# Moving four activation tensors in SBUF: split activations placed right behind the weight rings

## The reference, cut to what matters

```python
for i in range(DEPTH):
    g = norm_g[i]
    x = x + 0.5 * rmsnorm(swiglu(rmsnorm(x, g[0]), ffn1_wg[i], ffn1_wu[i], ffn1_wd[i]), g[1])
    xn = rmsnorm(x, g[2])
    ...                                   # y = the layer's mixer of xn
    x = x + rmsnorm(y, g[3])
    x = x + 0.5 * rmsnorm(swiglu(rmsnorm(x, g[4]), ffn2_wg[i], ffn2_wu[i], ffn2_wd[i]), g[5])

def swiglu(x, wg, wu, wd):                # D_MODEL 1024, D_FF 2816
    return (jax.nn.silu(x @ wg) * (x @ wu)) @ wd
```

## Time and profile before

| | |
|---|---|
| time, median of 3 runs | 2140.94 us (2139.95 to 2141.46) |
| span of the profiled execution | 2140.2 us |
| granted TensorE clock, mean over the span | 0.997 |
| TensorE matmuls, busy | 2108.0 us (98%), 14636 instructions |
| VectorE, busy | 1185.7 us (55%) |
| ScalarE, busy | 965.4 us (45%) |
| DMA, mean over the span | 180 GB/s |

### The profile page before, as it was taken

How to read it: one execution, slowest core, us unless ns; L and a number is a source line. 1 busy time by engine, 2 the same in 40 slices (tenths; PEclk the granted TensorE clock), 3 DMA queues, 4 the chain that set the end, 5 groups by cost and what they waited for, 6 DMA issues and landing times.

```text
span 2140.2 us, 35887 instructions
## 1 busy us (share of the span) xinstructions
PE 2108.0 (98%) x14636; PEld 1931.7 (90%) x14636; DVE 1185.7 (55%) x1346; ACT 965.4 (45%) x1177; POOL 52.5 (2%) x100
## 2 busy tenths in 40 slices
PE   8999999999998999999999999999999999999998
PEld 6998989988998998997999899898999899898997
DVE  5555765456456554555645654555645654576543
ACT  5444544344435544454444543554444543544442
POOL 0000000000000000000000000000000000000000
PEclk9999999999999999999999999999999999999999
DMA  8554655546554342342644545453644555455551
GB/s 317 185 191 167 221 185 203 206 160 216 194 185 172 124 153 100 119 158 94 232 186 179 206 187 203 153 193 134 231 185 178 205 188 203 154 212 187 205 187 60
DMA packets 55981, 386.27 MB, mean 180 GB/s; under 512 B 6592, under 2 KB 7104, under 8 KB 10816
## 3 DMA queue, kind: packets, MB, share of 16 engines
q1 hardware_dynamic: 52416, 372.53, 47.2%
q10 hardware_dynamic: 3456, 12.13, 1.6%
HBM read 383.58 MB, written 1.05 MB: 180 GB/s over the span
## 4 chain that ended last, share of the span: by engine, by line
PE 98%; ACT 1%; DVE 0%; issue 0%; DMA 0%; POOL 0%; POOLq 0%; ACTq 0%; DVEq 0%
PE ps L407 29%; PE ps L409 29%; PE ps L408 29%; PE ps L420 2%; PE ps L423 2%; PE ps L426 2%; PE ps L687 1%; PE ps L712 1%; PE ps L700 1%; PE ps L442 1%; PE ps L689 0%; PE ps L674 0%; PE ps L714 0%; ACT xT_high L905 0%; PE ps L497 0%
## 5 line engine op out<-in xcount | busy, mean ns | idle before, releaser
L1219 DVE TENSOR_TENSOR w_low<-raw,w_high 128x2048 fp32r<-128x2048 f32 x352 | 804.2, 2289 | 321.3 <-ACT w_high L881 321.1
L407 PE MATMUL ps<-xT_high,w_high 128*128 128x256 f32 x2656 | 736.0, 277 | 0.0
L409 PE MATMUL ps<-xT_high,w_low 128*128 128x256 f32 x2656 | 734.9, 277 | 0.0
L408 PE MATMUL ps<-xT_low,w_high 128*128 128x256 f32 x2656 | 734.5, 277 | 0.0
L881 ACT ACTIVATE w_high<-raw 128x2048 fp32r<-128x2048 f32 x352 | 670.7, 1911 | 37.7 <-DMA raw<-stream 21.1
L408 PEld LDWEIGHTS ps<-xT_low,w_high 128*128 128x128 f32 x2656 | 499.4, 188 | 2.7
L407 PEld LDWEIGHTS ps<-xT_high,w_high 128*128 128x128 f32 x2656 | 499.0, 188 | 3.1
L409 PEld LDWEIGHTS ps<-xT_high,w_low 128*128 128x128 f32 x2656 | 498.6, 188 | 0.0
L916 ACT ACTIVATE region<-ps 128x256 f32<-128x256 f32 x176 | 67.6, 384 | 668.6 <-PE ps L409 651.3
L407 PE MATMUL ps<-w_high,oT_hi 128*128 128x512 f32 x832 | 330.4, 397 | 0.0
L409 PE MATMUL ps<-w_high,oT_lo 128*128 128x512 f32 x832 | 329.6, 396 | 0.0
(11 more groups left out here) (147 smaller groups left out, 1258.3 us busy)
## 6 DMA issues: line engine op xcount, KB each, us to landing
raw<-stream SPq DMA_DIRECT2D x352, 1024.0 KB, 4.8
gain<-gains ACTq DMA_DIRECT2D x23, 512.0 KB, 4.7
x<-x_in SPq DMA_DIRECT2D x2, 512.0 KB, 6.0
out<-x SPq DMA_DIRECT2D x2, 512.0 KB, 2.6
gain<-gains SPq DMA_DIRECT2D x1, 512.0 KB, 5.3
att_mask<-att_mask_in SPq DMA_DIRECT2D x1, 384.0 KB, 5.1
rope<-rope_in SPq DMA_DIRECT2D x1, 128.0 KB, 4.5
ml_mask<-ml_mask_in SPq DMA_DIRECT2D x1, 128.0 KB, 4.9
```

What stands on the lines that cost most here:

```text
L407: nc.tensor.matmul(acc, lh, rh, start=start, stop=False)
L408: nc.tensor.matmul(acc, lh, rl, start=False, stop=False)
L409: return nc.tensor.matmul(acc, ll, rh, start=False, stop=stop)
L1219: nc.vector.tensor_tensor(w_low[:, p % RING, :], raw[:, p % RAW, :], w_high[:, p % RING, :], ALU.subtract).then_inc(piece_split, 1)
```

## The change

The four `sb` calls of the split activations are moved up, right behind the two rings. Nothing else is touched: every instruction, wait and loop stays as it is, and only addresses differ.

```diff
         w_high = sb("w_high", [P, RING, PIECE], F32R)
         w_low = sb("w_low", [P, RING, PIECE], F32R)
 
+        xT_high = sb("xT_high", [P, KD, SEQ], F32R)
+        xT_low = sb("xT_low", [P, KD, SEQ], F32R)
+        oT_hi = sb("oT_hi", [P, KD, SEQ], F32R)
+        oT_lo = sb("oT_lo", [P, KD, SEQ], F32R)
         x = sb("x", [P, TILES, D])
...
         minus_half = sb("minus_half", [P, 1])
-        xT_high = sb("xT_high", [P, KD, SEQ], F32R)
-        xT_low = sb("xT_low", [P, KD, SEQ], F32R)
         ident = sb("ident", [P, P])
...
         gate_bias = sb("gate_bias", [P, 2 * NH])
-
-        oT_hi = sb("oT_hi", [P, KD, SEQ], F32R)
-        oT_lo = sb("oT_lo", [P, KD, SEQ], F32R)
```

## The result

| | before | after |
|---|---|---|
| time, median of 4 runs | 2140.44 us (2139.72 to 2141.46) | 2178.68 us (2177.45 to 2179.35) |
| ratio after / before, 95% interval | | 1.0175 (1.0162 to 1.0188) |
| span of the profiled execution | 2140.2 us | 2176.6 us |
| granted TensorE clock, mean | 0.997 | 0.997 |

The changed kernel is 1.75% slower. I had forecast 2127 us and a range up to 2172; the time lies above both.

What follows compares the result with a forecast made beforehand. TensorE's matmuls, busy 2108.0 of 2140.2 us, were taken to bound the kernel as a sum of pitches. Down kind -13.5 us, all else 0, gave 2126.7 for the profiled execution, stated as 2127; range 2106 to 2172.

Steps and rivals of the forecast that it cites:

- Block kind: 7968 matmuls streaming 256 columns of `xT` over stationary weights: stays at 113.3 ns, 0 us.
- all turn slow: Upper bound for the 7968 block matmuls: each 4.5 ns slower, 35.9 us more.
- The four steps of 120 ns: Block kind's first four steps after a down product, 0.48 us before settling; cited for rival C.
- down kind: 2496 matmuls, 512 weight columns streaming, `oT` stationary: 234.2 to 228.8 ns, 13.5 us less; lower bound 226.6 ns.
- token kind: 2256 matmuls, 256 weight columns streaming, `xT` stationary: stays slow, 0 us; bounds 10.2 us less to 0.
- early kind: 768 matmuls, 512 weight columns streaming, `xT` stationary: stays at 228.8 ns, 0 us; bounds 1.7 less to 4.1 more.
- VectorE, ScalarE, clock: Engines writing `xT` and `oT` at new places: 0 cost, over 40% of span free; clock was full in every slice.
- Rival C: Load and stream meet at a common start, holding the block kind slow: 2175 us, or 2162 with down gain; chance 0.30.
- Rival A: Common starts settle everything: down and early kinds at 226.6 ns, token kind fast; 30.9 us less, 2110 us; chance 0.16.
- Rival B: Nothing changes; the down kind's 5.4 ns belong to something other than the offset: 2140.9 us; chance 0.20.
- the skill's rule: TensorE never waits on another SBUF user and weight loads take no read bandwidth, so no address can matter.

Runs made afterwards that it cites:

- e1: Kernel before with only `oT` moved behind the rings (`xT` offset 192, `oT` 0): 2149.36 us, ratio 1.0043 to before.
- e3: Changed kernel with pads ahead of `xT` and `oT`, putting `xT` at offset 192 and `oT` at 0: 2150.46 us, ratio 1.0043 to before.
- e2: Kernel before with only `xT` moved behind the rings (`xT` offset 0, `oT` 352): 2195.53 us, ratio 1.0251 to before.
- t_e1: e1 plus one float32 transpose between a down product and the following block at 64 places: 2130.81 us, ratio 0.9952 to before.
- best_both192: Changed kernel with one 192-byte pad ahead of `xT`, so `xT` and `oT` both sit at offset 192: 2132.10 us, ratio 0.9964 to before.
- t_after: Changed kernel plus one float32 transpose between a down product and the following block at 64 places: 2187.52 us.

## Why the prediction was wrong

**The step that failed** is "Block kind, 7968 matmuls, nearly all at 113.3 ns: left at that, 0, since the two paces come with one address and the address alone does not pick." It measured +47.9 us. The observation in it is right, both paces do come with one address, and e1 shows that the stream ahead picks between them; the conclusion is not. The offset decides which paces there are to pick from: 113.3 and 117.8 ns at 192, but 120.0 ns only at 0, in 332 of 332 halves. My bound above fell with it: "all turn slow", 35.9 us, took the slowest pace seen for the slowest there is, though I had written three paragraphs earlier that no pair in the trace starts in common. The four steps of 120 ns on coming from `down` were no warning of it: over all 64 such places the first four average 118.0, and they do settle. No row of the trace before gave the price of 6.7 ns.

**The down kind** went as forecast, and further: -13.5 us forecast, -16.1 measured (-17.7 in e1), a steady 226.7 ns in place of 228.8. That is the lower bound I gave, 226.6, and 19 us less would go with it; the changed kernel gets 16.1, in good part because the first five steps behind a block take 27 ns more than the steady pace there, and nothing more in e1. The direction, the 391 ns and the reason (offset of the stationary tensor) held; e1 and e3 show it.

**The token kind** was given 0 and bounds from -10.2 to 0. It took +5.4, since 117.8 became 120.0, outside the bounds for the same reason. Some 0.4 of this is on 144 matmuls of `arriving` with 256 columns, which my sum had left out.

**The early kind**: 0 forecast, -0.8 measured, inside its bounds; its steady pitch fell from 228.9 to 226.7 like the down kind's. **VectorE, ScalarE, clock**: no change, as said; the four terms make the whole span.

**Rival C** (2162 or 2175, chance 0.30) had the place and the sign. Its price was too small: 4.5 ns where 6.7 were paid. Its reason, that a load and a stream meet because they start in common, is not borne out: offsets 96 and 128 cost the block kind as much. **Rival A** (everything settles) had the 512-column kinds right and the 256-column kinds with the wrong sign. **Rival B**, and with it my reading of the skill's rule as one by which no address can matter, is out: only addresses differ, and the ratio is 1.0175 (1.0162 to 1.0188).

**A coupling that no case of mine had** shows in e1: the gain of the down kind costs the block kind its fast pace. Even with `xT` left alone my number would have been wrong: 2149, not 2127. The forecast comes nearest to the layout 192 and 192 (2132.10; -11.8 us on the down kind), which takes the down kind only to 228.9.

## What to carry to other kernels

When TensorE is full and an edit only moves tensors, take the pitch for each kind of operand pair (type, width, which side streams) at its own offset, and treat an offset that the trace does not have as unknown in both directions for the kind with the most matmuls; the slowest pace seen is not a bound. "Aligned" is neither good nor bad as such: the offset that gave the best 512-column pitch gave a 256-column one as slow as any, so try a few offsets of each stationary or streamed tensor by itself. Look at the pace behind each change of kind as well, because a quicker stream can hand a slower pace to the next.

## What the runs showed of the hardware that I had not expected

- The pitch of fp32r matmuls with a new stationary operand each time depends on the offset between moving and stationary operand: 113.3 to 120.0 ns with 256 columns (`xT` at 0, 96, 128, 256 and 384: 120.0; at 32: 116.7; at 64 and 192: 113.3 or 117.8), and from 226.7 to 234.3 ns with 512, at a granted clock of 1.00. It repeats at 256 bytes in the offsets tried (0 and 256, 128 and 384, 32 and 288, 96 and 352). By the Trainium skill, "SBUF — State Buffer", section "SBUF: two separate sides", TensorE never waits on another user of the SBUF. The runs agree as far as other engines go, 120.2 ns with them idle and 120.0 with one at work. They show that the places of TensorE's own two operands matter all the same: in e2 against before, `xT` is the only operand of the four kinds whose offset to the rings differs, 1.0251 (1.0234 to 1.0268). Whether it is the read of the weights or something else in the array that loses the 6.7 ns is not shown.
- At offset 192 a 256-column stream has two paces and keeps the one it starts in. Behind a down product with a pitch of 228.9, 233.3 or 234.3 ns it was 113.3 in 64 of 64 first halves, behind one of 226.7 ns 117.8 in 64 of 64. A 128-column fp32r matmul in between did not change that. A plain float32 transpose did, in t_e1 (74 of 75 places). It does not pick the pace alone: at the 11 places where every kernel has transposes ahead of a block, with `xT` at 192, between 4 (best_both192) and 11 (`oT` at 288) came out at 113, and two traces of one kernel (192 and 192) differ at 3 of them. What carries the pace is open.
- A float32 transpose between two fp32r streams costs more than itself: in t_e1, over 64 places, 28 ns to the next start and 202 ns for the step after it, in place of 118. t_after is 8.8 us longer than after, 138 ns for each of its 64 transposes.
